# Second block: the differential heads' score and output products and the retention heads' score products go from fp32 to pairs of f16 numbers

## The reference, cut to what matters

```
aq, ak, av, ag, bq, bk, bv, bg, cu, cg = split(h @ w_in)
# differential attention, 4 heads, two maps m of 64 channels, values 128 wide
logits[h,m] = q[h,m] @ k[h,m].T / 8 + bias[h]            # 512 x 512
p = softmax(logits);  attn = p[h,0] - lam * p[h,1];  o_a[h] = attn @ v[h]
# retention, both directions, 4 heads of 64 channels, values 128 wide
o_b[h] = ((rot(q[h]) @ rot(k[h]).T / 8) * decay[h]) @ v[h]
# pooling over windows of 2, 4, 8, 16 tokens, then a 128 x 128 product
x = x + concat(rms(o_a)*silu(ag), rms(o_b)*silu(bg), o_c*silu(cg)) @ w_out
```

## Time and profile before

| | before |
|---|---|
| median of 3 runs | 2670.35 us (2670.31 to 2670.37) |
| span of the profiled execution, first to last instruction | 2668.5 us |
| TensorE busy | 2656.6 us (100%) |
| VectorE busy | 1822.5 us (68%) |
| ScalarE busy | 1337.7 us (50%) |
| TensorE clock granted, mean | 0.999 |
| chain that ended last | TensorE 97% |

### The profile page before, as it was taken

One profiled execution on the slowest core, in us unless ns is written; L12 is line 12 of the kernel. 1 busy time (PEld: TensorE's weight loads), 2 busy tenths in 40 slices (PEclk: granted clock), 3 DMA queues, 4 the chain that ended last, 5 costly groups with the idle time before them and its releaser, 6 DMA issues.

```text
span 2668.5 us, 45121 instructions
## 1 busy us (share of the span) xinstructions
PE 2656.6 (100%) x17772; PEld 1741.6 (65%) x17772; DVE 1822.5 (68%) x2792; ACT 1337.7 (50%) x2284; POOL 136.5 (5%) x119
## 2 busy tenths in 40 slices
PE   9999999999999999999999999999999999999999
PEld 6886476654688646886476654688646556465664
DVE  7995385666899528994385665899526786557854
ACT  5664265552566425663265542566424654336452
POOL 1000012100100001000022100100000002000020
PEclk9999999999999999999999999999999999999999
DMA  5443321223344333443322223444323232321312
GB/s 170 115 121 107 122 80 59 88 67 104 91 120 116 116 98 95 121 115 107 122 80 67 81 74 104 116 125 111 121 100 119 72 95 72 111 84 64 111 64 87
DMA packets 313358, 266.23 MB, mean 100 GB/s; under 512 B 8796, under 2 KB 276316, under 8 KB 312576
## 3 DMA queue, kind: packets, MB, share of 16 engines
q1 hardware_dynamic: 310192, 254.31, 30.8%
q10 hardware_dynamic: 2416, 7.84, 1.1%
q0 software_dynamic: 608, 2.11, 0.3%
HBM read 257.40 MB, written 4.21 MB: 98 GB/s over the span
## 4 chain that ended last, share of the span: by engine, by line
PE 97%; DVE 1%; DMA 0%; DVEq 0%; ACT 0%; SPq 0%; issue 0%; ACTq 0%
PE pu L473 15%; PE pu L475 15%; PE pu L474 15%; PE pm L473 6%; PE pm L475 6%; PE pm L474 6%; PE pu L596 6%; PE pu L598 6%; PE pu L597 6%; PE pm L596 2%; PE pm L598 2%; PE pm L597 2%; PE pm L912 2%; PE pm L668 2%; PE pm L898 1%; PE pm L926 1%
## 5 line engine op out<-in xcount | busy, mean ns | idle before, releaser
L1105 DVE SCALAR_TENSOR_TENSOR w_lo<-stage,w_hi 128x2048 f16<-128x2048 f32 (+1 forms) x152 | 342.9, 2256 | 367.0 <-ACT w_hi L1885 363.3
L1885 ACT ACTIVATE w_hi<-stage 128x2048 f16<-128x2048 f32 (+1 forms) x143 | 265.9, 1859 | 529.4 <-PE pm L475 377.9
L473 PE MATMUL pu<-h_hi,w_hi 128*128 128x512 f16 x912 | 346.3, 380 | 0.0
L475 PE MATMUL pu<-h_hi,w_lo 128*128 128x512 f16 x912 | 345.6, 379 | 0.0
L474 PE MATMUL pu<-h_lo,w_hi 128*128 128x512 f16 x912 | 345.6, 379 | 0.0
L473 PE MATMUL pu<-w_hi,arena 128*128 128x512 f16 x512 | 194.0, 379 | 0.0
L474 PE MATMUL pu<-w_lo,arena 128*128 128x512 f16 x512 | 194.0, 379 | 0.0
L475 PE MATMUL pu<-w_hi,arena 128*128 128x512 f16 x512 | 194.0, 379 | 0.0
L473 PE MATMUL pm<-w_hi,arena 128*128 128x512 f16 x512 | 194.0, 379 | 0.0
L474 PE MATMUL pm<-w_lo,arena 128*128 128x512 f16 x512 | 194.0, 379 | 0.0
L475 PE MATMUL pm<-w_hi,arena 128*128 128x512 f16 x512 | 194.0, 379 | 0.0
(11 more groups left out here) (345 smaller groups left out, 6222.4 us busy)
## 6 DMA issues: line engine op xcount, KB each, us to landing
stage<-in_w_in_dram SPq DMA_DIRECT2D x144, 512.0 KB, 4.5
stage<-in_w_ffn_gate_dram SPq DMA_DIRECT2D x88, 512.0 KB, 3.9
stage<-in_w_ffn_up_dram SPq DMA_DIRECT2D x88, 512.0 KB, 5.1
stage<-in_w_ffn_down_dram SPq DMA_DIRECT2D x80, 512.0 KB, 4.0
stage<-in_w_out_dram SPq DMA_DIRECT2D x40, 512.0 KB, 4.2
stage<-in_w_ffn_down_dram SPq DMA_DIRECT2D x16, 256.0 KB, 4.2
stage<-in_w_branch_hgrn_dram SPq DMA_DIRECT2D x8, 512.0 KB, 3.4
stage<-in_w_branch_attn_dram SPq DMA_DIRECT2D x8, 512.0 KB, 4.6
```

What stands on the lines that cost most here:

```text
L473: nc.tensor.matmul(ps, w1, r_hi, start=first, stop=False)
L475: return nc.tensor.matmul(ps, w2, r_hi, start=False, stop=last)
L1105: V.scalar_tensor_tensor(out=w_lo[:, s, 0:n], in0=stage[:, s, 0:n], scalar=WSCALE, in1=w_hi[:, s, 0:n], op0=ALU.mult, op1=ALU.subtract).th ...
L1885: A.activation(w_hi[:, s, 0:n], stage[:, s, 0:n], ACT.Copy, scale=WSCALE).then_inc(hi_split, 1)
```

## The change

The queries, keys and values of the differential heads are written as f16 pairs (high, low) when their units are read out: ScalarE writes the high part from PSUM (`part_hi`), and `evacuate2` on VectorE waits for it and writes the low part. `scores2` makes three f16 matmuls for each map, maps alternating, where it made one in fp32; the scale comes off in the bias addition. `taken` copies the transposed block to a new fp32 buffer `wide` (which releases `pt_ready`), then writes `AT_hi` from it; VectorE writes `AT_lo` in a new `probs_low`. `head_out2` makes 48 f16 matmuls of 128 columns where it made 16 in fp32. The rotated retention queries and keys are split the same way (ScalarE the high, VectorE the low part, in two halves), and retention's scores are three f16 matmuls each. Retention's output products stay in fp32.

```diff
+SPLIT2 = ("aq", "ak", "av")
+SS = 1.0 / (ASCALE * ASCALE)
...
+        AT_hi, AT_lo = f16(93.25, NB, T), f16(97.25, NB, T)
+        wide = gp[:].rearrange("p (a b) -> p a b", a=2)
...
             def scores2(i):
                 hd, b = divmod(i, NB)
-                for m in (1, 0) if i in (8, 12) else (0, 1):
+                parts = (daq_hi, dak_hi), (daq_hi, dak_lo), (daq_lo, dak_hi)
+                def part(m, j):
+                    r = slice(64 * m, 64 * m + 64)
+                    return nc.tensor.matmul(pm[2 * (i % 2) + m][:], parts[j][0][r, hd, b * P:(b + 1) * P], parts[j][1][r, hd], start=j == 0, stop=j == 2)
+                order = (1, 0) if i in (8, 12) else (0, 1)
+                for m in order:
                     if m == 0 and i >= 2:
                         pe.wait_ge(pt_ready, t.at("pt_ready", i - 1))
...
-                    last = nc.tensor.matmul(pm[2 * (i % 2) + m][:], daq[r, hd, b * P:(b + 1) * P], dak[r, hd], start=True, stop=True)
+                    last = part(m, 0)
+                for j in (1, 2):
+                    for m in order:
+                        last = part(m, j)
                 last.then_inc(sc_done, 1)
...
+            def head_out2(ps, v_hi, v_lo, hd):
+                pairs = (AT_hi, v_hi), (AT_hi, v_lo), (AT_lo, v_hi)
+                for b in range(NB):
+                    for kb in range(NB):
+                        for j, (l, r) in enumerate(pairs):
+                            last = nc.tensor.matmul(ps[:, b * P:(b + 1) * P], l[:, kb, b * P:(b + 1) * P], r[:, kb, hd * P:(hd + 1) * P],
+                                                    start=kb + j == 0, stop=kb == NB - 1 and j == 2)
...
             def retention_scores(hd):
...
+                for i in (0, 2):
+                    for e in range(2):
...
+                        score(i + e, 0)
+                    for e in range(2):
+                        score(i + e, 1)
+                    for e in range(2):
+                        score(i + e, 2).then_inc(ret_done, 1)
...
             def mixer2_slot(q):
 
                 if q in (5, 9, 13, 17):
 
-                    pe.wait_ge(pt_ready, t.next("pt_ready", 4))
-                    pe.wait_ge(p_ready, t.now("p_ready"))
+                    t.next("pt_ready", 4)
+                    pe.wait_ge(pt_lo, t.next("pt_lo", 4))
...
+            def probs_low(i):
+                v.wait_ge(pt_hi, t.next("pt_hi"))
+                c = slice(i % NB * P, (i % NB + 1) * P)
+                V.scalar_tensor_tensor(out=AT_lo[:, :, c], in0=wide[:, i % 2].rearrange("p (k c) -> p k c", k=NB), scalar=ASCALE, in1=AT_hi[:, :, c],
+                                       op0=ALU.mult, op1=ALU.subtract).then_inc(pt_lo, 1)
...
-                    for z, table in ((bqk, K_COS), (swapped, K_SIN)):
-                        V.tensor_tensor(z, z, cst[:, table:table + T].unsqueeze(1).to_broadcast([P, 4, T]), ALU.mult)
+                    for c in range(2):
+                        for z, table in ((bqk, K_COS), (swapped, K_SIN)):
+                            V.tensor_tensor(z[:, c:4:2], z[:, c:4:2], cst[:, table:table + T].unsqueeze(1).to_broadcast([P, 2, T]), ALU.mult)
+                        v.drain()
+                        V.tensor_tensor(rotated[:, c:4:2], bqk[:, c:4:2], swapped[:, c:4:2], ALU.add).then_inc(rot_pre, 1)
                     v.drain()
-                    V.tensor_tensor(bqk, bqk, swapped, ALU.add).then_inc(rot_ready, 1)
+                    for c in range(2):
+                        v.wait_ge(rot_hi, t.next("rot_hi"))
+                        V.scalar_tensor_tensor(out=turned_lo[:, c:4:2], in0=rotated[:, c:4:2], scalar=ASCALE, in1=turned_hi[:, c:4:2],
+                                               op0=ALU.mult, op1=ALU.subtract).then_inc(rot_ready, 1)
...
                 between()
+                if q in (4, 8, 12, 16):
+                    probs_low(q - 1)
                 if q < 16:
                     probs2(q)
+                    if q not in (0, 4, 8, 12):
+                        probs_low(q - 1)
...
                     v.wait_ge(unit_done, t.next("unit_done"))
+                if kind in SPLIT2:
+                    v.wait_ge(part_hi, t.next("part_hi"))
+                    for out_hi, out_lo, bank, scale in halves2(kind, part, banks):
+                        last = V.scalar_tensor_tensor(out=out_lo, in0=bank, scalar=scale, in1=out_hi, op0=ALU.mult, op1=ALU.subtract)
+                    last.then_inc(evac, 1)
...
-                A.activation(AT[:, :, b * P:(b + 1) * P], pm[2 * (i % 2)][:].rearrange("p (k c) -> p k c", k=NB), ACT.Copy).then_inc(pt_ready, 1)
+                if i >= 2:
+                    s_.wait_ge(pt_lo, t.at("pt_lo", i - 1))
+                A.activation(wide[:, i % 2], pm[2 * (i % 2)][:], ACT.Copy).then_inc(pt_ready, 1)
+                s_.drain()
+                A.activation(AT_hi[:, :, b * P:(b + 1) * P], wide[:, i % 2].rearrange("p (k c) -> p k c", k=NB), ACT.Copy, scale=ASCALE).then_inc(pt_hi, 1)
...
             def mixer2(l):
                 hi_after_tail()
                 for n, (kind, part) in enumerate(MIX2_ORDER):
+                    if kind in SPLIT2:
+                        banks = ((set_a, pu)[l] if n < 2 else pu)[2 * (n % 2):2 * (n % 2) + 2]
+                        s_.wait_ge(unit_done, t.now("unit_done") + 1)
+                        for out_hi, _, bank, scale in halves2(kind, part, banks):
+                            last = A.activation(out_hi, bank, ACT.Copy, scale=scale)
+                        last.then_inc(part_hi, 1)
```

More of the change, by code:

```diff
@@ L345, in build_program @@
         rot_ready = sem("rot_ready")
+        part_hi = sem("part_hi")
+        pt_hi = sem("pt_hi")
+        pt_lo = sem("pt_lo")
+        rot_hi = sem("rot_hi")
+        rot_pre = sem("rot_pre")
         rot_land = sem("rot_land")
@@ L362, in build_program, with halves2 @@
         end_half = sem("end_half")
+        def halves2(kind, part, banks):
+            dst = {"aq": (daq_hi, daq_lo), "ak": (dak_hi, dak_lo), "av": (dV_hi, dV_lo)}
+            out_hi, out_lo = dst[kind]
+            scale = DS * ASCALE * (0.125 if kind == "aq" else 1.0)
+            if kind in ("av", "bv"):
+                cols = slice(part * 256, part * 256 + 256)
+                return [(out_hi[:, b:b + 2, cols], out_lo[:, b:b + 2, cols], banks[b // 2][:].rearrange("p (b c) -> p b c", b=2), scale) for b in (0, 2)]
+            return [(out_hi[:, 2 * part + e], out_lo[:, 2 * part + e], banks[e][:], scale) for e in range(2)]
         x_in = a["x"].rearrange("(b p) d -> p b d", p=P)
@@ L954, in mixer2_slot @@
                         pe.wait_ge(rot_ready, t.next("rot_ready", 2))
+                    if hd == 2:
+                        pe.wait_ge(rot_ready, t.next("rot_ready"))
                     if hd < B_HEADS:
@@ L1656, in softmax2 @@
                 for m in range(2):
-                    V.tensor_tensor(Lm[:, m], pm[2 * (i % 2) + m][:], toep[:, hd, first:first + T], ALU.add)
+                    V.scalar_tensor_tensor(out=Lm[:, m], in0=pm[2 * (i % 2) + m][:], scalar=SS, in1=toep[:, hd, first:first + T], op0=ALU.mult, op1=ALU.add)
                 v.drain()
@@ L2239, in mixer2_slot @@
                     s_.wait_ge(o_done, t.next("o_done"))
[L2240 removed]
+                    A.activation(tc[:, k % 2], ps[:], ACT.Copy, scale=SS if k < A_HEADS else 1.0).then_inc(o_sq, 1)
                 if 1 <= q <= 16 and q not in (8, 12):
@@ L2247, in mixer2_slot @@
                 if q == 18:
-                    s_.wait_ge(rot_ready, t.at("rot_ready", 2))
+                    for c in range(2):
+                        s_.wait_ge(rot_pre, t.next("rot_pre"))
+                        A.activation(turned_hi[:, c:4:2], rotated[:, c:4:2], ACT.Copy, scale=ASCALE).then_inc(rot_hi, 1)
+                    s_.wait_ge(rot_ready, t.at("rot_ready", 3))
                     for g in range(2):
-                        A.dma_start(swapped[64 * g:64 * g + 64], bqk[64 * (g ^ 1):64 * (g ^ 1) + 64]).then_inc(dup_land, 16)
+                        A.dma_start(swapped_both[64 * g:64 * g + 64], turned_both[64 * (g ^ 1):64 * (g ^ 1) + 64]).then_inc(dup_land, 16)
                 if q == 17 or (0 <= ret < B_HEADS - 1 and step == 0):
```

35 lines of the change are left out of this document (21 added, 14 removed).

## The result

| | before | after |
|---|---|---|
| median | 2670.34 us (4 runs, 2670.31 to 2670.37) | 2690.42 us (4 runs, 2686.22 to 2693.39) |
| span of the profiled execution | 2668.5 us | 2684.4 us (a run of 2686.22 us) |
| TensorE busy | 2656.6 us | 2642.3 us |
| TensorE clock granted, mean | 0.999 | 0.997 in the profiled run, 0.993 to 0.995 in the other three |

The ratio is 1.0074, 95% interval 1.0062 to 1.0086: slower by 20 us. The profiled run is the shortest of the four; that the others are longer is part of the finding. The mean clock is a rough guide only: the kernel before shows 0.998 to 1.000 in runs that agree within 0.1 us. The mean also holds stretches at lower clock at the very start (0.57 from 9.5 to 13.5 us of the kernel before) and at the very end, where TensorE does nothing (0.50 from 2665.4 us).

What follows compares the result with a forecast made beforehand. TensorE, busy for the whole span, was taken as the bound. Its savings against waits of 14.8 us a layer made each layer 6.1 longer, two layers 12: span 2680.5, with 1.8 around it 2682.4 us; range 2662 to 2694.

Steps and rivals of the forecast that it cites:

- The chain and the `part_hi` wait: VectorE's low parts wait for ScalarE's high parts behind the exponentials; slots 0 and 2 grow to 8.79 and 10.63 us.
- The addition slot by slot: Starts of scores groups, carried on from TensorE's and VectorE's slot lengths; group 15 at 121.8 us after group 0.
- 10 of it from the three `part_hi` waits: Of TensorE's 14.8 us of waits a layer, 10 come from the high-part waits in slots 0, 2 and 6.
- TensorE's waits, 14.8 us a layer: TensorE's new waits before scores groups and transpositions in the differential heads' slots, 14.8 us a layer.
- The scores group: Three f16 pairs take 0.65 us instead of 0.86: 0.21 saved a group, 32 groups, 6.8 us.
- The output product: 48 f16 matmuls of 128 columns at 0.056 us: 2.68 instead of 3.57, eight products, 7.1 us saved.
- Retention's scores: In f16, head 0 saves 0.84 us and heads 1 to 3 save 0.43 each; 2.1 a layer, 4.2 in all.
- The waits hold nobody: Rival: the three high-part waits cost nothing and TensorE's saving stays; faster, 2662 us; chance 0.15.
- F16 halves don't overlap: Rival: f16 matmuls on different row halves don't overlap, each scores group 0.43 us longer; 2697 us; chance 0.07.
- The waits run deeper: Rival: drains and signals longer than 0.1 us, or an output product of 3.9; 2690 to 2694 us; chance 0.08.

Runs made afterwards that it cites:

- experiment 4: The changed kernel with matmuls of ones, results unused, put where TensorE waits before scores groups 2, 4 and 8; 2687.14 us.
- experiment 1: The changed kernel with ScalarE writing the high parts of aq1, ak1 and av1 before the exponentials of slots 0, 2 and 6; 2669.65 us.
- experiment 9: The kernel of experiment 8 with the high parts of aq1 and ak1 back behind the exponentials of slots 0 and 2; 2670.61 us.
- experiment 10: The kernel of experiment 8 with retention's queries, keys and scores back in fp32; 2660.83 us.
- experiment 2: The changed kernel with `probs_low` moved from VectorE to GpSimd, high parts still behind the exponentials; 2682.33 us.
- experiment 3: The changed kernel with high parts written before the exponentials and `probs_low` on GpSimd; 2663.66 us.
- experiment 8: The kernel of experiment 1 with values, probabilities and output products back in fp32, scores of both kinds of heads still f16; 2657.19 us.
- experiment 7: The kernel of experiment 1 with retention's rotation, scores and scale back in fp32; 2667.59 us.

## Why the prediction was right, and where it was off

The forecast was 2682 us (2682.4 in the sum), slower, in 2662 to 2694; it came out at 2690.42, slower. The reason is the one given. The size missed by 8 us: just outside the 2676 to 2690 that had most of the chance, and inside the range only by its upper part, which was there for longer waits and not for what filled it. Some 1.7 us of the 8 are terms of the sum that missed on both sides, the rest is the clock, as far as the traces tell.

- **The chain and the `part_hi` wait.** The addition slot by slot held. Forecast and measured starts of the groups, from group 0: 2: 15.0 and 14.7; 4: 33.0 and 32.5; 6: 49.6 and 49.1; 8: 67.2 and 68.0; 10: 84.3 and 85.3; 15: 121.8 and 122.4; the fourth product 137.1 and 137.5. Farthest off are 9 (73.8 and 76.1) and 12 (98.5 and 100.2), behind the first fall of the clock. That the product comes out within 0.4 is partly luck: with the clock up (experiment 4) it starts at 136.4. VectorE's slots 0 and 2: 8.79 and 10.63 forecast, 8.61 and 10.47 measured. The shares are shown, not only argued, by experiments 1 and 9: "10 of it from the three `part_hi` waits" is 9.9 us at the fourth product (137.5 less 127.6), 8.8 of them without the clock's 1.1.
- **TensorE's waits, 14.8 us a layer.** The waits view gives 13.8 up to the fourth product (its first three rows). It counts each from the modelled end of the matmul ahead, 0.165 us (0.38 less 0.215) after the point where the next could have started; with ten waits that is 15.4, against 14.8.
- **The scores group was mis-sized.** "0.21 saved" is 0.31 (1.06 less 0.754). The f16 halves do overlap. If the three pairs take the 0.65 of the forecast, only 0.1 of the 0.2 taken as fixed stays. Over 32 groups that is 9.8 us and not 6.8, and experiment 10, which contains this term almost alone, gained 9.6.
- **The output product** is 2.68, as forecast, and 56 ns a matmul: with the rule of the Trainium skill ("TensorE: Matmul & The Clock Gate", section on the back-to-back issue gap), some 81 ns in such a stream, it would by an estimate have been 3.9. The trace disagrees with it.
- **Retention's scores.** Heads 1 to 3 save 0.52 each (1.920 to 1.402; forecast 0.43). Head 0 saves 0.21 instead of 0.84: 0.6 of the rest is a wait inside it, for the copy of the turned head.
- **Missed: what stands behind the second copy and the rotation.** Groups 8 and 12 also need `copy_scale`, which ScalarE does after the copy to `AT_hi`: group 8 started 4.8 us later than a slot without waits would have it, where I had 3.6. And the turn in slot 19 waits 1.2 for `scale_head`, behind VectorE's longer rotation. So the layer ended 7.9 longer (pooling at 220.7, before 212.8), 6.8 without the clock's 1.1, where I had 6.1. I had followed the wait to the next scores group, not to each other buffer that the same engine hands over.
- **Missed: the clock.** Three stretches at half clock take 5.1 us of TensorE's time in the profiled run and cost it about 2.1 (experiment 4); without them it would have taken 2684.1, against a forecast of 2682.4 in the sum. The other three runs are 4.2 to 7.2 us longer still, at a mean clock lower by 0.002 to 0.004; that these are further such stretches is an inference, since they have no trace, and the mean does not order them (0.993 at 2690.38 us, 0.994 at 2693.39). This step was not in the sum at all. I had priced an idle TensorE at the time that it idles.
- **The rivals.** "The waits hold nobody": experiment 1 takes them away and stands at 2666.4 in its fastest runs, where that rival had 2662; its remaining waits are 7.9 us a layer, not 4.8, and the scores group saves more than that rival had. "F16 halves don't overlap" is refuted by 0.754. "The waits run deeper" (2690 to 2694) has the right time by another mechanism: drains and signals were as taken, the clock was not.

What stays open: when the clock falls. The same waits did not always bring it down. A wait of 2.65 us before group 4 of the changed kernel was followed by no fall in the first layer and by one in the second. At retention's first scores, with a wait of about 1.2 us before the turn and 0.55 inside head 0, it fell in both layers of experiment 4, in the second alone of experiments 1 and 2 (0.8 and 0.55 there), and in neither of the changed kernel and of experiment 3 (0.9 and 0.55). It did not fall in experiment 8, with the 0.55 alone, nor in experiments 7 and 10, with neither wait; each of these is one traced run, but their runs agree within 0.4 us. What part the f16 scores on half of the rows have in it, no run here tells: none has them without a wait inside head 0, and none has these waits without them.

## What to carry to other kernels

When a read-out is split between two engines, look at where the first half lands in that engine's order, not at its length: 1.1 us of ScalarE's work put behind two exponentials instead of ahead of them cost 13 to 21 us here. Price every f16 split by what it asks of the engines in the chain: the scores' split puts little into the softmax slots, the scale in an instruction that was there and the high parts in two of them, and paid 13 us with retention's; the probabilities' split puts a copy and a subtraction into each, to save 0.9 us of TensorE in every fourth, and cost 7 to 12. And where a TensorE that was never idle begins to wait, add a term for its clock.

## What the runs showed of the hardware

- **A wait can cost more than its length.** The granted clock fell to half for 3.4 or 6.8 us after waits of 3.41 us (group 8) and also of 2.00 (group 4 of experiment 9), in a stretch that was otherwise busy. Not every such wait was followed by it (a wait of 2.65 us before group 4 was not in the first layer of the changed kernel, and was in the second). The changed kernel's runs span 7.2 us, those of experiments 7 and 8 less than 0.3. A spread like that in a kernel on one core was itself the sign.
- **Half clock costs what the critical path sees of it**: 1.7 us of TensorE's time in 3.4 us, of which 1.1, and in one place nothing, was left at the fourth product where VectorE held later slots; 3.0 us for 6.8 at the retention scores, by the time of the pooling (experiment 4).
- **Work put into the gap went with a clock that stayed up** (experiment 4), at no cost to the chain: groups 2, 4 and 8 started when they had. In one traced run no fall was left at the three filled places in either layer; whether the kernel gains by it is not shown, since the clock fell elsewhere.
- **VectorE beside GpSimd**: a two-input instruction of 0.75 us took 1.64 where GpSimd subtracted two arrays of 512 columns beside it, and GpSimd's subtraction took 1.65 where it took 1.16 in the next slot.
- **f16 matmuls on 64 rows**: six of 512 columns on alternating halves take 0.754 us to the next start, where four fp32 records took 1.06.
